# Sharing the low-part subtractions of the mixing layer's weights between VectorE and GpSimd

## What is computed

```python
h = h + 0.5 * swiglu(rmsnorm(h, norm_ffn1), ffn1_w_in, ffn1_w_out)
u = rmsnorm(h, norm_mix)
proj = u @ w_in          # 1024 x 11,312: z | x,B,C | dt | q | k | v | forget | two gates
o_ssm  = Mamba-2 SSD(z, conv(x,B,C), dt)      # 32 heads, 8 groups, state 128, chunked scan
o_attn = forgetting attention(q, k, v, log f) # 16 heads
merged = sigmoid(g_ssm) * (o_ssm @ w_br_ssm) + sigmoid(g_attn) * (o_attn @ w_br_attn)
h = h + merged @ w_out
h = h + 0.5 * swiglu(rmsnorm(h, norm_ffn2), ffn2_w_in, ffn2_w_out)
```

## Time and profile before

| | us |
|---|---|
| median of three runs | 1967.37 |
| lowest and highest | 1964.48, 1967.89 |
| the profiled execution, its own time | 1968.98 |
| its span, first to last instruction | 1967.2 |

### The profile page before, as it was taken

The page is one execution under the profiler, slowest core; times in us unless marked ns, Lnnn a source line. Parts: engine busy times, 40 slices in busy tenths (PEclk is TensorE's granted clock), DMA queues, the critical chain, the costliest instruction groups (busy, mean ns, idle before and its releaser), DMA issues. The chain is left out here.

```text
span 1967.2 us, 35664 instructions
## 1 busy us (share of the span) xinstructions
PE 1915.3 (97%) x14329; PEld 1866.2 (95%) x14329; DVE 1197.9 (61%) x1858; ACT 942.1 (48%) x1804; POOL 561.7 (29%) x598
## 2 busy tenths in 40 slices
PE   7999999998999999999999999999999999999997
PEld 7999999997999999999999899999999999999997
DVE  5696776867663466346634662223454879687774
ACT  6253343535665566556655664333222445344343
POOL 2020211105744264426441643223101212021210
PEclk9999999998999999999999999999999999999999
DMA  5233323342216131612161225225433223333231
GB/s 139 71 94 94 87 86 87 91 125 81 86 60 205 35 92 58 210 35 86 60 212 36 84 62 174 86 65 164 128 98 119 65 88 102 91 86 98 76 105 50
DMA packets 227506, 190.51 MB, mean 97 GB/s; under 512 B 11153, under 2 KB 215249, under 8 KB 226193
## 3 DMA queue, kind: packets, MB, share of 16 engines
q1 hardware_dynamic: 222384, 173.94, 29.6%
q0 software_dynamic: 3616, 11.90, 2.0%
q10 hardware_dynamic: 1344, 2.43, 0.4%
HBM read 168.89 MB, written 19.33 MB: 96 GB/s over the span
## 5 line engine op out<-in xcount | busy, mean ns | idle before, releaser
L2116 PE MATMUL ps<-xah,wh 128*128 128x296 f32 (+1 forms) x1728 | 384.4, 304 | 10.1 <-DVE wl L1822 4.2
L2116 PE MATMUL ps<-xah,wl 128*128 128x296 f32 (+1 forms) x1728 | 383.8, 304 | 0.0
L2116 PE MATMUL ps<-xal,wh 128*128 128x296 f32 (+1 forms) x1728 | 378.3, 300 | 0.0
L1003 POOL TENSOR_TENSOR wl<-raw,wh 128x512 fp32r<-128x512 f32 (+1 forms) x184 | 232.5, 1271 | 406.3 <-ACT wh L1126 406.0
L2116 PEld LDWEIGHTS ps<-xah,wh 128*128 128x128 f32 x1728 | 279.9, 190 | 11.8 <-DVE wl L1822 4.4
L2116 PEld LDWEIGHTS ps<-xal,wh 128*128 128x128 f32 x1728 | 281.1, 190 | 0.0
L2116 PEld LDWEIGHTS ps<-xah,wl 128*128 128x128 f32 x1728 | 279.9, 190 | 0.1
L2182 PE MATMUL ps<-xth,wh 128*128 128x288 f32 (+1 forms) x640 | 190.0, 297 | 1.7 <-DVE wl L1686 1.7
L2182 PE MATMUL ps<-xth,wl 128*128 128x288 f32 (+1 forms) x640 | 190.0, 297 | 0.0
L2182 PE MATMUL ps<-xtl,wh 128*128 128x288 f32 (+1 forms) x640 | 189.8, 296 | 0.0
L944 POOL TENSOR_TENSOR sums<-raw 128x512 f32<-128x512 f32 x40 | 52.4, 1311 | 390.2 <-DMA raw<-in_ffn_w_in_dram 212.5
(11 more groups left out here) (344 smaller groups left out, 4670.5 us busy)
## 6 DMA issues: line engine op xcount, KB each, us to landing
raw<-in_ffn_w_in_dram SPq DMA_DIRECT2D x87, 512.0 KB, 5.1
raw<-in_w_in_dram SPq DMA_DIRECT2D x80, 512.0 KB, 4.7
raw<-in_ffn_w_out_dram SPq DMA_DIRECT2D x48, 384.0 KB, 3.7
brow<-acs_rows SPq DMA_DIRECT2D x8, 1184.0 KB, 6.1
raw<-in_w_br_ssm_dram SPq DMA_DIRECT2D x16, 512.0 KB, 4.0
bias<-bias_rows SPq DMA_DIRECT2D x32, 160.0 KB, 5.6
os_spill<-yT SPq DMA_DIRECT2D x8, 592.0 KB, 3.0
bias<-biasp_rows SPq DMA_DIRECT2D x16, 264.0 KB, 6.1
```

What stands on the lines that cost most here:

```text
L1003: ins = pool.tensor_tensor(wl[:, slot, k, 0:cols], raw[:, slot, k, 0:cols], wh[:, slot, k, 0:cols].bitcast(F32), ALU.subtract)
L2116: ins = pe.matmul(bank(b + a, half), as_row(w)[:, at + 256 * k + j * P:at + 256 * k + (j + 1) * P], x[:, k, a * half:(a + 1) * half], star ...
```

## The change

`shared(n, c)` is now true for c = 0 and c = 2 of every duo of the mixing layer. So VectorE makes the lower parts of the first and third quarter, 96 in all, and GpSimd those of the second and fourth, also 96. Before, VectorE had 8 and GpSimd 184. For the 128-column duos VectorE now takes 128 columns as GpSimd did. `key_split`, signalled after VectorE's third quarter, is now waited for by TensorE before every such duo (but the first of all, whose weights were split earlier) and once after the loop, and by SyncE before every load into a split slot.

```diff
 def shared(n, c):
-    return MID[n] == "q1" and c % 2 == 0
+    return c % 2 == 0
...
                     if kind == "split" and step[2] == 3:
+                        sp.wait_ge(key_split, dve_splits.up())
                         if MID[g] == "q1":
-                            sp.wait_ge(key_split, now + 1)
                             sp.sem_inc(cleared, 1)
...
                         if shared(g, c):
                             dve.wait_ge(hi_part, hparts())
                             k = slice(2 * c, 2 * c + 2)
-                            ins = dve.tensor_tensor(wl[:, s, k, :], raw[:, s, k, :], wh[:, s, k, :].bitcast(F32), ALU.subtract)
+                            cols = split_cols(g)
+                            ins = dve.tensor_tensor(wl[:, s, k, 0:cols], raw[:, s, k, 0:cols], wh[:, s, k, 0:cols].bitcast(F32), ALU.subtract)
                             if c == 2:
                                 ins.then_inc(key_split, 1)
...
                         if t == 0:
                             duo_split()
-                            if k == "k":
-                                pe.wait_ge(key_split, i + 1)
+                            if not (steps is FIRST_STEPS and n == 0):
+                                pe.wait_ge(key_split, dve_splits.up())
...
+            pe.wait_ge(key_split, dve_splits.up())
```

More of the change, by code:

```diff
@@ L878, in mid @@
                         sp.sem_inc(heads_left, 1)
+            dve_splits = Count()
             for n in range(3):
```

## The result

The changed kernel takes **1985.95 us** (median of three runs, 1984.86 to 1987.3) against 1967.37: a ratio of 1.0095, 95% interval 1.008 to 1.0109, 18.6 us slower. The forecast was 18.3 us. The sum came out, but several of its terms did not; what follows goes by the terms.

A forecast was written before the change was run, and what follows sets the result against it. TensorE, busy 97%, bounds the kernel, so only its waits count. The terms 3.0 + 6.8 + 3.4 + 5.1 + 0.8 + 0.4 + 0.8 - 1.2 - 0.8 = 18.3 us on 1967.37 gave 1985.7 us; 8-in-10 range 1974 to 1995.

The forecast's parts named there:

- The bound: Whole kernel: TensorE is busy 97%, so only its waits move the time; 61 us more on VectorE is no time by itself.
- The opening, +3.0: Before the `tstack` copies: the c = 2 subtraction waits for ScalarE's upper part, so `tstack` ends later, +3.0 us (2.4 to 4.5).
- the 8.7 that the prediction named as a sign: Opening: if the forecast is right, TensorE's waits list `tstack` with about 8.7 us.
- z, c = 2: Scans' z duos: the subtraction before `cbm` of tile 0 makes TensorE wait, 1.7 us four times, +6.8 us.
- v, c = 2: Scans' v duos: the same delay of `cbm` with a half-size quarter, 0.85 us four times, +3.4 us.
- The attention: Three windows, x and bc duos: c = 2 +0.75 us each, c = 0 about +0.1 each, +5.1 us; quarters before first scores free.
- z and v, c = 0: First quarters at the z and v duos: z +0.2 us four times, +0.8; v +0.1 four times, +0.4.
- q0: Two half-size quarters among tightly timed tiles: 0.1 us each, eight times, +0.8 us.
- The gains: Waits for `mb` -0.3 us four times, -1.2 (bounds -2.4 and 0); for `yg` -0.2 each, -0.8 (bounds -1.6 and 0).
- The clock: Rival: the new 1.7 and 0.85 us waits lower TensorE's clock and cost more than they last, giving 1999 us; chance 0.10.
- Relief wins: Rival: ScalarE's upper parts come before VectorE reaches them, `mb` and `yg` waits go, giving 1963 or 1960 us; chance 0.05.
- Balance: Rival: VectorE's idle share and slack at `cb` hide the cost, gains and losses balance, 1967 +- 3.9 us; chance 0.08.

The follow-up runs named there:

- the version with later places: Changed kernel with the same 96 lower parts on VectorE, 26 of them issued later, behind the steps they stood in front of: 1958.7 us, 0.9953 to the kernel before.
- the thin one: Changed kernel with VectorE making only 16 of 256 (or 128) columns of each moved quarter and GpSimd the rest: 1989.89 us, 1.0113 to the kernel before.
- the gain alone: Kernel before with only eight quarters moved to VectorE, c = 0 beside the scans' x and bc duos: 1964.34 us, ratio 0.9982.

## Why the forecast held, point by point

**The bound.** Right: TensorE stays 97% busy, and all of the time went where it waits. 61 us of work on VectorE was no time by itself; the version with later places has all of it and is faster than before.

**The opening, +3.0.** Its total held by luck: two terms came out larger than given, one smaller. From the scan that makes `tsum` to its last instruction for `tstack` VectorE took 4.2 us before and 8.2 after, not 7.1: the step that failed is "the copies 0.45 + 0.46", where the first took 1.54. Without GpSimd beside it that stretch is 7.15 us, 2.9 more than before, which is the forecast's figure for ScalarE's readiness. In turn the two quarters beside the z duo did not "give back about as much" as they cost: they gave 1.6 us net. In the nine kernels where GpSimd no longer makes these two in full the scan begins 27.1 to 27.8 us after the start of the mixing layer, in the three where it does (before, the thin one, the gain alone) 29.1 to 29.2. The third term was not in the sum: 0.7 us in which TensorE works at the lower clock for longer (see the rivals). In sum, 4.0 - 1.6 + 0.7 = 3.1. The shorter wait for GpSimd, 1.8 us, was worth nothing, as said: TensorE comes to the wait for `tstack` 2.5 us sooner. That makes this wait 10.7 us, and not the 8.7 that the prediction named as a sign.

**z, c = 2.** It was 1.41 us of wait, 1.58 by the step, where 1.7 was taken; `xdd` beside it made the subtraction 0.92, inside the bound given. What the forecast lacked is the next tile: VectorE is late there too, by 0.36 more. In sum it is 7.0 against 6.8.

**v, c = 2.** Right: 0.87 against 0.85.

**The attention.** Right at x and bc, with 0.80 and 0.77 against 0.75 and 0.75. Wrong on both sides of it: the c = 0 quarters cost nothing, and the third quarter beside z, said to fall in idle time, costs 0.33 ahead of the first scores, where TensorE waits for `mx`.

**z and v, c = 0.** At z it was +0.20 as forecast, at v +0.25 for 0.1. Made behind the taps (the version with later places) they cost nothing at v, and z gains two steps over before, 0.46 and 0.36, which is about the 0.9 us by which the taps exceeded their own time; 0.21 of it comes back where the scan's second `mb` is due. **q0.** It cost 0, where 0.8 was taken.

**The gains.** The mechanism held and the size did not: "about half come back at the next tile" was wrong for `mb`, where 0.77 us came and stayed (the wait alone was 0.6). They came to -3.1 and -1.5 us against -1.2 and -0.8, the first beyond the bound of -2.4. VectorE is 1.3 us faster there, and that is not spent by the tile after.

So the mechanism held, and part of the closeness of the total is luck: gains sized too small (2.6 us) and losses at places held for free (0.36 and 0.33, 2.4 us in all) balanced, and the table's 16.5 comes up to the measured 18.6 only with 2.1 us that it does not list.

**The rivals.** The clock is told by the stretches' granted clock (us of the stretch, busy us and instructions of PE, PEld, DVE, ACT, POOL, then PEclk). The kernel before, behind the 3.0 us wait and around the end of the 5.8 us wait:

```profile
459.30:462.60 3.30, 3.30 (x15) 3.30 (x14) 3.19 (x5) 2.42 (x5) 2.03 (x4) 0.50 0.94 310
...
476.40:483.10 6.70, 5.82 (x20) 4.26 (x21) 6.43 (x12) 3.55 (x10) 2.49 (x2) 0.50 0.27 68
```

The changed kernel:

```profile
455.00:474.00 19.00, 12.75 (x92) 11.93 (x90) 16.02 (x22) 9.87 (x16) 9.66 (x11) 1.00 0.17 56
474.20:487.70 13.50, 7.41 (x27) 5.85 (x28) 8.76 (x15) 5.03 (x14) 1.26 (x1) 0.50 0.35 95
...
443.00:497.00 54.00, 40.70 (x276) 38.11 (x277) 40.34 (x56) 30.56 (x58) 20.45 (x20) 0.87 0.27 79
...
500.00:700.00 200.00, 194.37 (x1483) 182.84 (x1482) 108.61 (x281) 113.38 (x280) 61.79 (x80) 1.00 0.31 94
```

In 500 to 700 us, with the new waits of 1.4, 1.1 and 0.7 us in it, the clock is 1.00: waits of that length did not lower it, and the rival is false in the form given. In the opening it holds in a small way. Behind the wait for GpSimd, now 1.8 us, the clock no longer falls, which is worth nothing as TensorE then waits for `tstack`. Around the end of the 10.7 us wait it is at the lower level (1.2 GHz) from 474.1 to 487.8. TensorE works 7.5 us of that, from 480.3 on, where it worked 5.9 us before, from 477.3 to 483.2. That is the 0.7 us, and the 0.87 instead of 0.91.

Relief wins: false in the form given, as ScalarE's readiness decided the named places. It is late there by more than the prediction's "0.2 to 2.6 us": the rows give 2.6, 2.4 and, in the opening, 2.8 us; the 0.2 belongs to the attention's bc duo. Yet the relief that this rival spoke of is real, 11.4 us by the kernel that leaves the work out, and a small shift in order collects most of it. Balance: false.

## What to carry to other kernels

Before work is moved to an engine that issues in order, ask of each place when its input is ready against when the instructions behind it are needed, and add the work's own time to that, rather than add up the work alone: here 18 badly placed instructions of 0.4 to 0.7 us cost 22 us, and the same instructions behind the urgent one turned 0.9% slower into 0.5% faster. Move the work, and then move its place too. And look for the gain beyond the waits that TensorE's list names: leaving the moved work out altogether was the shortest way to see how much there was.

## What was not expected of the hardware

A VectorE copy of one 32x592 SBUF operand, which takes 0.45 us, took 1.54, 1.46 and 1.43 us beside a GpSimd subtraction, and 0.52 when that was made small. The exclusion that the earlier trace rows show for two SBUF inputs holds for this copy too. The Trainium skill, page "SBUF — State Buffer", section "Who interferes with whom", has it: a copy can run in a two-port mode and then contends, though an instruction with at most one SBUF input outside these modes does not; the trace agrees with the first half, and whether the copy ran in such a mode no run here shows.

The exclusion works in the other direction as well: GpSimd's `zt`, 0.86 us at its place in the z duo before, took 1.30 beside VectorE's subtraction in the version with ScalarE's upper part earlier.

The relief reached TensorE at places where its list of waits names ScalarE and "issue". In the kernel before, ScalarE's timeline of the z duo shows how (tanh, then `zr`):

```profile
502.77 0.70 ACT L1456 ACTIVATE th<-cvt 128x595 f32<-128x595 f32 x1 [2.32 <-DVE cvt L1940]
...
503.64 0.38 ACT L1385 ACTIVATE zr<-ps 128x256 f32<-128x256 f32 x1
```

`zr`, for which TensorE waits 0.3 us four times, stands on ScalarE behind a tanh that waits 2.32 us for the taps, and the taps were stretched by GpSimd. With the 88 subtractions off GpSimd, and VectorE's behind the taps, the two steps there gained 0.46 and 0.36 us in each of the four rounds.
